# A chunked state scan on TensorE: products paired over four array quarters, state products moved into the level loop, and the unit matrix of X0 replaced by a second T1 product

## What is computed

```
def rwkv7_scan(r, w, k, v, a, b):
    def step(state, inp):
        r_t, w_t, k_t, v_t, a_t, b_t = inp
        sa = einsum('bhvk,bhk->bhv', state, a_t)
        state = state * w_t + sa[..., None] * b_t + v_t[..., None] * k_t
        return state, einsum('bhvk,bhk->bhv', state, r_t)
    ...
    _, out = lax.scan(step, zeros(b, h, 64, 64), xs)      # 256 steps
```

## Time and profile before

| | us |
|---|---|
| median of 3 runs | 1915.73 (1913.83 to 1916.65) |
| the profiled execution | 1913.86 |
| its span, first to last instruction | 1912.1 |
| of it the scan, first to last product of L1418 | about 110.2 (948.4 to 1058.6) |

### The profile page before, as it was taken

One profiled execution on the slowest core, in us unless ns is written; L12 is line 12 of the kernel. 1 busy time (PEld: TensorE's weight loads), 2 busy tenths in 40 slices (PEclk: granted clock), 3 DMA queues, 4 the chain that ended last, 5 costly groups with the idle time before them and its releaser, 6 DMA issues.

```text
span 1912.1 us, 31653 instructions
## 1 busy us (share of the span) xinstructions
PE 1847.4 (97%) x12631; PEld 1539.3 (81%) x12631; DVE 1117.7 (58%) x1166; ACT 808.4 (42%) x1091; POOL 1366.0 (71%) x683
## 2 busy tenths in 40 slices
PE   5999999999999999999899999999999999999998
PEld 1778878888668898888688678888888888788886
DVE  1116858560343546878654664788888888923334
ACT  3334444444454554344322544433333334333334
POOL 2657978888348889965443788999999989844443
PEclk8999999999999999999999999999999999999999
DMA  9994555555775565643100345656555555655552
GB/s 360 379 342 156 179 170 177 182 195 183 262 282 177 175 200 186 195 144 127 45 4 5 125 163 197 194 181 196 179 194 180 193 179 193 217 180 197 197 191 95
DMA packets 174431, 352.55 MB, mean 184 GB/s; under 512 B 6736, under 2 KB 19422, under 8 KB 171774
## 3 DMA queue, kind: packets, MB, share of 16 engines
q1 hardware_dynamic: 172940, 346.31, 54.1%
q10 hardware_dynamic: 1393, 4.83, 0.6%
HBM read 349.02 MB, written 2.10 MB: 184 GB/s over the span
## 4 chain that ended last, share of the span: by engine, by line
PE 65%; DVE 11%; POOL 9%; issue 9%; DMA 3%; ACT 2%; SPq 1%; POOLq 0%; DVEq 0%; ACTq 0%
PE bank L980 9%; POOL WL L589 8%; PE bank L920 8%; PE bank L921 8%; PE bank L925 8%; PE bank L987 5%; PE bank L1639 4%; PE bank L1632 4%; PE bank L1634 4%; PE bank L1418 3%; DMA arena<-in_w_ada 3%; PE bank L913 2%; DVE arena L2270 2%; PE bank L915 2%; PE bank L914 2%
## 5 line engine op out<-in xcount | busy, mean ns | idle before, releaser
L589 POOL TENSOR_TENSOR WL<-WR,WH 128x1024 fp32r<-128x1024 f32 (+2 forms) x514 | 1263.6, 2484 | 396.4 <-ACT WH L1683 395.5
L1683 ACT ACTIVATE WH<-WR 128x1024 fp32r<-128x1024 f32 (+2 forms) x556 | 570.4, 1036 | 738.5 <-PE bank L987 320.0
L980 PE MATMUL bank<-HX,WH 128*128 128x512 f32 x1840 | 461.5, 392 | 0.0
L980 PEld LDWEIGHTS bank<-HX,WH 128*128 128x128 f32 x1840 | 330.9, 189 | 59.1
L920 PE MATMUL bank<-WH,HX 128*128 128x512 f32 (+2 forms) x800 | 314.4, 394 | 4.1 <-ACT WH L1683 2.2
L921 PE MATMUL bank<-WH,HX 128*128 128x512 f32 (+2 forms) x800 | 306.3, 383 | 0.0
L987 PEld LDWEIGHTS bank<-HX,WL 128*128 128x128 f32 x1840 | 250.5, 190 | 22.0 <-POOL WL L589 4.6
L987 PE MATMUL bank<-HX,WL 128*128 128x256 f32 x1840 | 257.7, 283 | 1.1 <-POOL WL L589 0.6
L925 PE MATMUL bank<-WL,HX 128*128 128x512 f32 (+2 forms) x800 | 208.7, 382 | 0.6 <-POOL WL L589 0.6
L920 PEld LDWEIGHTS bank<-WH,HX 128*128 128x128 f32 x800 | 150.7, 188 | 36.8 <-issue 7.9
L921 PEld LDWEIGHTS bank<-WH,HX 128*128 128x128 f32 x800 | 150.9, 189 | 28.6 <-issue 2.2
(11 more groups left out here) (349 smaller groups left out, 2272.6 us busy)
## 6 DMA issues: line engine op xcount, KB each, us to landing
WR<-in_w_in SPq DMA_DIRECT2D x96, 1024.0 KB, 5.0
WR<-in_ffn_w_gate SPq DMA_DIRECT2D x44, 1024.0 KB, 5.1
WR<-in_ffn_w_up SPq DMA_DIRECT2D x44, 1024.0 KB, 5.2
WR<-in_ffn_w_down SPq DMA_DIRECT2D x42, 1024.0 KB, 5.0
arena<-in_w_ada SPq DMA_DIRECT2D x64, 512.0 KB, 10.4
WR<-in_w_out SPq DMA_DIRECT2D x32, 1024.0 KB, 5.0
WR<-in_w_ada SPq DMA_DIRECT2D x16, 1024.0 KB, 5.1
WR<-in_w_in SPq DMA_DIRECT2D x12, 768.0 KB, 4.4
```

The source lines that it names most:

```text
L589: eng.tensor_tensor(half(*low_of(n), *w), half(*raw_of(n), *w), half(*high_of(n), *w), ALU.subtract).then_inc(ready, 1)
L980: last = pe.matmul(BANK[(first + f) % 8][:, :].rearrange("p (h n) -> p h n", h=2), wh[:, k, f * P:(f + 1) * P], hx[:, :, kk, :], start=kk ...
L1683: act.activation(half(WH, nth(n) % 2, *w), half(WR, n % NSLOT, *w), ACT.Copy).then_inc(hi_ready, 1)
```

## The change

1. `four` becomes a generator `each`; `in_turn` takes one product each from two of them until both are used up.
2. The chunk's first products are all 64 columns wide and paired over four quarters: b·a with b·r, then a·b with k·r. k·a moves to level 5, where it is joined by the transposed v (AV). LBr and AKr become LOWr (b·a and k·a, below the diagonal) and UPr (b·r and k·r).
3. X0 is copied by DVE once, with its mask and without the unit matrix. T1 = M1·L + M1·I instead: two products for each tile.
4. Level 1's X and Z both go to ACT; V and level 5's Z too.
5. The state products move one level down and beside T: P1 with T2, U with T3, Y with T4, S with T5. Of P1, Y and S the column groups q = 0, 1 run in turn with T and the others after it. U runs whole beside T3.
6. After the last chunk P1 also follows alone, then U, then Y. ACT's four `HH` stay between P1 and U.
7. POOL makes M2 to M5 of both sets after both sets' Z0.

```diff
-                    for m in range(2, LEVELS):
+                for m in range(2, LEVELS):
+                    for s in range(2):
                         below_level(m, s, c)
...
+            def each(s, bank, c0, *terms, swap=False, qs=range(4)):
+                o = BANK[4 * s + bank][:, c0:c0 + 4 * N].rearrange("p (q n) -> p q n", q=4)
+                for q in qs:
                     for n, (x, y) in enumerate(terms):
                         for h, to in zip(halves, swapped if swap else halves):
-                            last = pe.matmul(o[to, q, :], x(h, q), y(h, q), start=(n == 0), stop=(n == len(terms) - 1))
+                            yield pe.matmul(o[to, q, :], x(h, q), y(h, q), start=(n == 0), stop=(n == len(terms) - 1))
...
+            def in_turn(one, other):
+                last = other_last = None
+                for x, y in zip_longest(one, other):
+                    last, other_last = (last if x is None else x), (other_last if y is None else y)
                 return last, other_last
...
+                r_, a_, b_, k_ = (chunk_of(v, c) for v in (RA[:, 0], KKn, Bv, RKV[:, 8:16]))
                 for s in range(2):
...
+                        A_.wait(pe, f"Z{LEVELS - 1}_{s}", c - 1)
+                    if c >= 2:
+                        DS_.wait(pe, f"Sum_{s}", c - 2)
+                    last, _ = in_turn(each(s, 2, 0, (of_set(b_, s), of_set(a_, s)), swap=True),
+                                      each(s, 1, 0, (of_set(b_, s), of_set(r_, s))))
+                    P_.mark(last, f"LB1_{s}")
+                    if c >= 1:
+                        D_.wait(pe, f"T{LEVELS - 1}_{s}", c - 1)
+                    last, upto_last = in_turn(each(s, 3, 0, (of_set(a_, s), of_set(b_, s)), swap=True),
+                                              each(s, 1, 4 * N, (of_set(k_, s), of_set(r_, s))))
+                    P_.mark(last, f"L_{s}")
+                    P_.mark(upto_last, f"KR_{s}")
...
+                    D_.wait(pe, f"L_{s}", c)
+                    L_.wait(pe, f"M1_{s}", c)
+                    P_.mark(four(s, 3, 0, (of_pair(LM[s][0]), of_pair(Xi[s])), (of_pair(LM[s][0]), unit)), f"T1_{s}")
...
+                    L_.wait(pe, f"Z0_{s}", c)
+                    D_.wait(pe, f"T1_{s}", c)
+                    level_xz(1, s, c)
+                    four(s, 2, 0, (of_set(b_, s), unit))
+                    P_.mark(four(s, 2, 4 * N, (of_set(k_, s), unit)), f"BK_{s}")
...
+                    x_last, z_last = in_turn(each(s, 0, 0, (z, t2), swap=m > 1), each(s, 1, 0, (t2, z), swap=m == 1))
+                    P_.mark(x_last, f"X{m}_{s}")
+                    P_.mark(z_last, f"Z{m}_{s}")
...
+                upto = lambda i: (lambda h, q: UPr[par][s][h, i, q, :])
+                k_below = lambda h, q: LOWr[par][s][h, 1, q, :]
+                tok = lambda i: (lambda h, q: BKt[par][s][h, (4 * i + q) * N:(4 * i + q + 1) * N])
+                r_, a_ = of_set(chunk_of(RA[:, 0], c), s), of_set(chunk_of(KKn, c), s)
+                state, u, v = of_pair(ST[s]), of_pair(Us[s]), of_pair(Vp[par][s])
+                if m == 2:
+                    return each(s, 2, 0, *([(a_, state)] if c else []), (k_below, v), qs=qs)
+                if m == 3:
+                    return each(s, 2, 4 * N, (of_pair(Zi[par][s]), of_pair(P1[s])), qs=qs)
+                if m == 4:
+                    return each(s, 2, 0, *([(state, r_)] if c else []), (u, upto(0)), (v, upto(1)), qs=qs)
+                return each(s, 2, 4 * N, (tok(0), u), (tok(1), v), qs=qs)
...
                 products(c)
-                for m in range(1, LEVELS):
+                for m in range(2, LEVELS):
                     for s in range(2):
                         L_.wait(pe, f"M{m}_{s}", c)
...
+                        A_.wait(pe, f"X{m - 1}_{s}", c)
+                        t = each(s, 3, 0, (of_pair(LM[s][m - 1]), of_pair(Xi[s])), swap=True)
...
+                            state_wait(m, s, c - 1)
+                            t_last, u_last = in_turn(t, state_part(m, s, c - 1, range(4) if m == 3 else range(2)))
+                        P_.mark(t_last, f"T{m}_{s}")
+                        if c >= 1 and m == 3:
+                            S_.mark(u_last, f"U_{s}")
+                    if m == LEVELS - 1:
+                        for s in range(2):
+                            if c >= 1:
+                                rest_of(m, s, c - 1)
+                        k_, a_, v_ = (chunk_of(v, c) for v in (RKV[:, 8:16], KKn, RKV[:, 16:24]))
+                        for s in range(2):
+                            four(s, 0, 0, (of_set(k_, s), of_set(a_, s)))
+                            P_.mark(four(s, 0, 4 * N, (of_set(v_, s), unit)), f"AV_{s}")
...
+                            rest_of(m, s, c - 1)
...
+                        if m == 2:
+                            A_.wait(pe, f"Z1_{s}", c)
+                        level_xz(m, s, c)
+            for m in (2, 3, 4):
+                for s in range(2):
+                    state_wait(m, s, NCH - 1)
+                    for last in state_part(m, s, NCH - 1):
+                        pass
+                    S_.mark(last, f"{STATE[m]}_{s}")
...
+            take_state(2, NCH - 1)
             for g in range(4):
                 act.activation(HH[:, 8 + 2 * g:10 + 2 * g, :], YMT[:, 2 * g:2 * g + 2, :], ACT.Copy).then_inc(y_hi, 1)
-            for m in (2, 3):
+            for m in (3, 4):
```

More of the change, by code:

```diff
@@ L13 @@
 from contextlib import ExitStack
+from itertools import zip_longest
 import numpy as np
@@ L1410, in _, with four @@
             chunk_of = lambda v, c: v[:, :, c * C:(c + 1) * C]
[L1412 to L1415 removed]
+            def each(s, bank, c0, *terms, swap=False, qs=range(4)):
+                o = BANK[4 * s + bank][:, c0:c0 + 4 * N].rearrange("p (q n) -> p q n", q=4)
+                for q in qs:
                     for n, (x, y) in enumerate(terms):
                         for h, to in zip(halves, swapped if swap else halves):
[L1418 to L1428 removed]
+                            yield pe.matmul(o[to, q, :], x(h, q), y(h, q), start=(n == 0), stop=(n == len(terms) - 1))
+            def four(*where, **how):
+                for last in each(*where, **how):
+                    pass
+                return last
+            def in_turn(one, other):
+                last = other_last = None
+                for x, y in zip_longest(one, other):
+                    last, other_last = (last if x is None else x), (other_last if y is None else y)
                 return last, other_last
@@ new lines, in _, with state_wait @@
+            STATE = {2: "P1", 3: "U", 4: "Y", 5: "S"}
+            def state_wait(m, s, c):
+                if m == 2:
+                    A_.wait(pe, f"V_{s}", c)
+                    D_.wait(pe, f"KA_{s}", c)
+                    if c >= 1:
+                        DS_.wait(pe, f"S_{s}", c - 1)
+                    if c < NCH - 1:
+                        A_.wait(pe, f"BK_{s}", c + 1)
+                    else:
+                        AS_.wait(pe, f"Y_{s}", c - 1)
+                elif m == 3:
+                    AS_.wait(pe, f"P1_{s}", c)
+                    A_.wait(pe, f"Z{LEVELS - 1}_{s}", c)
+                elif m == 4:
+                    AS_.wait(pe, f"U_{s}", c)
+                else:
+                    AS_.wait(pe, f"Y_{s}", c)
@@ L1491, in _, with rest_of @@
+            def rest_of(m, s, c):
+                for last in state_part(m, s, c, range(2, 4)):
+                    pass
+                S_.mark(last, f"{STATE[m]}_{s}")
             pe.wait_ge(ops_ready, 5)
@@ L2029, in _ @@
                 for s in range(2):
+                    take("X1", s, c, 0, 0, flat4(Xi[s]))
+                    take("Z1", s, c, 1, 0, flat4(Zi[c % 2][s]))
                     if c >= 2:
@@ L2032, in _ @@
                     take("BK", s, c, 2, 0, BKt[c % 2][s])
-                for s in range(2):
-                    take("V", s, c, 2, 0, flat4(Vp[c % 2][s]))
-                for m in range(1, LEVELS):
-                    if c >= 1 and m < 3:
-                        take_state(m, c - 1)
-                    if m < LEVELS - 1:
-                        for s in range(2):
-                            take(f"X{m}", s, c, 0, 0, flat4(Xi[s]))
-                    if c >= 1 and m == 3:
-                        take_state(m, c - 1)
-                    if c == NCH - 1 and m == 4:
-                        take_state(1, c)
+                for m in range(2, LEVELS):
+                    if c >= 1 and m < 5:
+                        take_state(m, c - 1)
+                    for s in range(2):
+                        if m < LEVELS - 1:
+                            take(f"X{m}", s, c, 0, 0, flat4(Xi[s]))
+                        else:
+                            P_.wait(act, f"AV_{s}", c)
+                            A_.mark(act.activation(flat4(Vp[c % 2][s]), BANK[4 * s][:, 4 * N:8 * N], ACT.Copy), f"V_{s}")
+                for s in range(2):
```

(4 more changed lines are left out.)

170 lines of the change are left out of this document (58 added, 112 removed).

## The result

The changed kernel takes 1924.88 us in the median of five runs (1922.94 to 1927.02), beside 1915.59 us of the kernel before: a ratio of 1.0052, 95% interval 1.0037 to 1.0066. A second set of five runs gave 1923.33 us and a ratio of 1.0042 (1.0028 to 1.0055). It is slower by 8 to 9 us. The forecast was 1921.0, within 1906 to 1929, with 0.53 for slower.

The account below looks back on a forecast made before the run. Instruction supply was taken to bound PE: 0.4 us plus 30.1 blocks x 3.75 us, plus 2.4 at the scan's end, gave 115.7 against 110.2; 5.5 us longer, median 1921 us, range 1906 to 1929.

Parts of the forecast that it names:

- The mechanism: In the scan, PE's instructions come in blocks of 256, one per 3.75 us, slower than the paired products' 2.9 us a block.
- Gaps released by "issue": Sign in the scan: PE stands 0.7 to 1.5 us at the end of almost every block, with no semaphore.
- The windows of one block: Sign in the scan: windows of 128 products take 3.5 to 4.0 us; under 3.3 us would prove the forecast wrong.
- the pairing is hidden wholly: In the scan, 13.1 us less PE issue from pairing shortens only what stands waiting for instruction supply.
- The interval: Time to supply one block of PE instructions in the scan: 3.75 us, bounds 3.45 to 4.0, for 30.1 blocks.
- The tail: End of the scan: Y waits for U behind ACT's HH copies, 6.4 us instead of 3.75; cost taken as 2.4.
- T1 behind POOL: At each chunk's start T1 waits for POOL's M1: nothing under supply, 5.2 us in all if supply is no bound.
- DVE and ACT: In the scan, their changed copies and the state's waits of 0.3 to 0.4 us before T cost nothing under supply.
- Supply hides, work decides: Rival: supply no bound in the scan, which takes 99.7 us, 10.5 less; kernel 1905 us; chance 0.17.
- Short blocks: Rival: scan blocks supplied at the short end, 3.45 us each giving 1912 us; chance 0.08 for under 3.45.
- The pairs don't pair: Rival: T and state products in the scan still run at 29 ns, 12 us more, 1928 us; chance 0.05.
- The clock falls: Rival: PE's standing in the scan drops the granted clock to 1.2 GHz, some 60 us more; chance 0.03.

Follow-up runs that it names:

- b_pad: The kernel before with 64 one-element products a chunk added whose results nobody reads, 1024 PE instructions in all: 1934.61 us, ratio 1.0101.
- a_x0: The changed kernel with X0's unit matrix added by DVE again and T1 as one product per tile: 1920.37 us, ratio 1.0028 to the kernel before.
- a_hh: The changed kernel with ACT's four HH copies behind U's copies at the scan's end: 1920.50 us, ratio 1.0031 to the kernel before.
- a_unpaired: The changed kernel with all pairs undone, one operation issued after the other, same products: 1921.56 us, ratio 1.0031 to the kernel before.
- a_xz: The changed kernel with only X and Z paired and its new pairs undone: 1922.88 us, ratio 1.0045 to the kernel before.
- b_unpaired: The kernel before with X and Z of levels 1 to 4 issued one after the other: 1915.29 us, ratio 0.9998.
- b_narrow: The kernel before with each 128-wide product split into two of 64, 512 instructions more: 1917.29 us, ratio 1.0011.
- after_again: The changed kernel run once more, unaltered, as a second set and profile: 1923.33 us, ratio 1.0042 to the kernel before.

## Why the prediction was right, and where it was off

**The mechanism held.** Instructions, blocks and packets: 7770, 30.3 and "some 31" forecast, 7762 and 31 found. Gaps released by "issue" after almost every block: at 23 of 31, three in four, and of 0.4 to 1.85 us where 0.7 to 1.5 was forecast. PE's busy share in the scan about 80%: 77%. The windows of one block were to take 3.5 to 4.0 us, and 18 of 29 did. The scan was to take 114 to 118 us, and both profiles of after lie above. b_pad, a_x0 and a_hh moved the scan by what blocks and tail are worth. That the pairing is hidden wholly was the boldest step, and a_unpaired, a_xz and b_unpaired bear it out: none of them shows a gain by pairs.

**The scan was forecast at 115.7 us and took 120.4 (119.0 in the second profile).** The terms:

- *The interval, mis-sized.* I took 3.75 us, the mean of nine windows of before, and bounds of 3.45 to 4.0. From 949.21 to 1062.50 the 29 intervals are 3.91 each: 29 x 0.16 = 4.5 us, nearly the whole miss. In the second profile they are 3.81, 29 x 0.06 = 1.6 us, so some 3 us of the miss are the execution's and not the order's. The split into three parts shows where the time lies: landing to issue is 1.4 us in every kernel, but the next packet started later, 1.37 us after the block's first instruction in the mean against 1.26 in the ten blocks of before that ended in a gap, and took 1.17 against 1.02. In the second profile the two are 1.32 and 1.10. Five of the 23 starts came 1.68 to 2.30 us late; with 1.3 in their place, 3.8 us would go. The nine windows of before were no clean measure of the supply either: three of them (from 965.61, 1014.61 and 1042.32) ended without a gap, so PE's work set their length, and the ten that did end in one are 3.69 in the mean. What makes a packet start late is open: the number of instructions begun by then is 67 to 199, with no order that I could find.
- *The tail.* 2.4 forecast. The last full interval is 5.83 us, 1.9 over the mean, and moving HH gave 1.9. The gap before Y was 1.9 us where "some 2" was forecast.
- *T1 behind POOL, nothing.* Once it showed, in the second chunk: 1.0 us, in one of the waits above, at the end of a block of 3.88 us. It was covered only in part: the packet of the next block had landed 1.96 us before that block's first instruction, 0.56 more than the usual 1.4, so about half a us of the wait counted.
- *DVE and ACT, nothing.* DVE has no entry in PE's list; ACT's in the scan, besides the tail, add up to 1.2 us, all within blocks that ended in a gap.

In terms of before: three more intervals of 3.91 are 11.7, the tail 1.9, and the other 27 intervals fell from 4.03 to 3.91, -3.2: 10.4 us, against 10.3 measured. The last of these is mostly the wide products' six slow blocks (5.04 to 5.28 us each), which did go.

**The rivals.** *Supply hides, work decides* (1905): refuted for the changed kernel, by the gaps and by a_unpaired. It was the Trainium skill's rule ("Runtime: NRT & Kernel Launch", section "Instruction fetch mechanics") that pointed there; it says that fetches stay hidden. The trace agrees with its block of 256 and with the fetch of the next during the current one, and disagrees with the result: 23 visible waits. *Short blocks*: no, 3.91 and 3.81. *The pairs don't pair*: refuted, the first 128 products of after, paired, take 1.88 us, 14.7 ns each:

```profile
949.04:950.92 1.88, 1.88 (x128) 1.88 (x128) 0.99 (x3) 0.00 (x0) 0.53 (x1) 1.00 0.67 254
...
982.72:983.26 0.54, 0.54 (x34) 0.54 (x38) 0.00 (x0) 0.00 (x0) 0.54 (x2) 1.00 0.11 30
```

T with the state's products keeps that pace: in a stretch of 0.54 us in which a product of T and one of the state take turns, 34 of them run, 16 ns each (second row). *The clock falls* was given 0.03 as a lasting state. It does fall, but for 3 to 4 us at a time:

```profile
965.00:966.00 1.00, 0.82 (x27) 0.83 (x27) 0.23 (x1) 0.00 (x0) 0.00 (x0) 0.99 0.00 0
966.00:967.00 1.00, 1.00 (x35) 0.85 (x35) 0.62 (x2) 0.00 (x0) 0.00 (x0) 0.50 0.08 16
967.00:968.00 1.00, 1.00 (x48) 1.00 (x42) 0.43 (x1) 0.38 (x1) 0.00 (x0) 0.50 0.00 0
968.00:969.00 1.00, 1.00 (x32) 1.00 (x26) 0.42 (x1) 0.38 (x1) 0.00 (x0) 0.50 0.00 0
969.00:970.00 1.00, 1.00 (x40) 1.00 (x39) 0.63 (x2) 0.00 (x0) 0.00 (x0) 0.80 0.00 0
```

That block took 4.30 us without a gap; against an interval of 3.8 to 3.9 the fall cost 0.4 to 0.5 us.

## What to carry to other kernels

Before speeding up a stream of small products, count the engine's instructions and compare its pace with that of its supply: here 256 instructions per 3.8 to 3.9 us, so 15 ns each, or 30 ns for a product and its load. Below that, packing products closer buys nothing, and an edit that adds instructions to spare another engine an operation costs what they weigh in blocks; fewer instructions for the same work are what helps (a_x0, and b_narrow from the other side). When work is taken out, look for the wait on another engine that it had covered: cutting unread products and moving AK took 1 us off the scan, and 5 together with POOL's order.

## What the runs showed of the hardware

- PE's instructions come one block of 256 ahead, not more: the packet for the next block never started earlier than 0.2 us before the first instruction of the current one, and in blocks that end in a gap the three parts of the interval are 1.2 to 1.5, 1.0 to 1.2 and 1.4 us in the mean, in all the kernels run. The Trainium skill ("Runtime: NRT & Kernel Launch", section "Instruction fetch mechanics") gives PE a store of 2048 instructions; no run here shows more than the block in work and the next.
- In a block whose work is long, the next one's packet is in time and costs nothing. That is the block of before from 998.10 to 1003.17, 5.07 us with wide products, whose packet lies in the fourth of 40 slices, half a us after its start:

```profile
DMA  0005000000000000000000000000000000000000
GB/s 0 0 0 129 0 0 0 0 0 0 0 0 0 0 0 0 0 0 0 0 0 0 0 0 0 0 0 0 0 0 0 0 0 0 0 0 0 0 0 0
```

- The granted clock fell to 0.50 within the scan of after, a_hh (twice), after_again and b_pad (twice), each time 0.9 to 2.8 us after the start of a pause of PE of 1.5 to 2.1 us, three times before that pause was over, and was back 3.4 us later. It did not fall after every such pause (1.81, 1.85 and, before Y, 1.88 us in after left it at 1.00), so a pause of that length is no sufficient cause.
- The same kernel's scan differs from one execution to another: 120.4 and 119.0 us for after, with mean intervals of 3.91 and 3.81 us and a fall of the clock at different places. One profile settles a mechanism, not a difference of 2 to 3 us.

Not tried: 128-wide products paired over four quarters, which would give PE more work for each instruction; whether four quarters pay in that form is open.
